# Two-layer mixer and expert network on one core: three weight matrices of the second expert loaded into slots beside the ring, and gate biases summed in the out stage

## What is computed

```
cond = silu(c)
for layer in range(2):
    mod = cond @ ada_w[layer] + ada_b[layer]
    sh_m, sc_m, gt_m, sh_f, sc_f, gt_f = split(mod, 6)
    h = modulate(rms_norm(x, norm_mix[layer]), sh_m, sc_m)
    x = x + gt_m * mixer(h)            # even_mixer, then gla_mixer
    h = modulate(rms_norm(x, norm_ffn[layer]), sh_f, sc_f)
    x = x + gt_f * hier_moe(h)         # top-1 group of 4, top-2 experts in it
# one expert:
hid = silu(h @ w1[e]) * (h @ w3[e]);  y = hid @ w2[e]
```

## Time and profile before

| | |
|---|---|
| median of 3 runs | 2037.02 us (2034.14 to 2037.91) |
| profiled execution, its own time | 2039.77 us |
| its span, first to last instruction | 2037.9 us |
| TensorE busy | 1689.9 us (83%) |
| VectorE, ScalarE busy | 607.2 us (30%), 362.7 us (18%) |
| moved by the DMA engines | 582.33 MB, mean 286 GB/s |
| mean granted TensorE clock | 0.917 of 2.4 GHz |

### The profile page before, as it was taken

How to read it: one execution, slowest core, us unless ns; L and a number is a source line. 1 busy time by engine, 2 the same in 40 slices (tenths; PEclk the granted TensorE clock), 3 DMA queues, 4 the chain that set the end, 5 groups by cost and what they waited for, 6 DMA issues and landing times.

```text
span 2037.9 us, 26620 instructions
## 1 busy us (share of the span) xinstructions
PE 1689.9 (83%) x11304; PEld 1049.5 (51%) x11304; DVE 607.2 (30%) x1546; ACT 362.7 (18%) x817; POOL 74.1 (4%) x80
## 2 busy tenths in 40 slices
PE   6997879877676776999986866786789999899988
PEld 4756754433333333755543533353368884558753
DVE  2657643211111111671321111111142051411192
ACT  1013113100000001222320100000021132311271
POOL 0000100000000001000000000000100000000000
PEclk8997898988888888998898988898899999999999
DMA  9995206999999999764499999999994433046100
GB/s 354 377 295 207 83 2 248 403 428 429 427 429 428 429 428 415 266 238 154 176 417 422 426 429 428 426 427 427 427 337 150 143 139 145 1 149 227 61 1 31
DMA packets 142767, 582.33 MB, mean 286 GB/s; under 512 B 30941, under 2 KB 42333, under 8 KB 117985
## 3 DMA queue, kind: packets, MB, share of 16 engines
q1 hardware_dynamic: 113504, 558.49, 68.0%
q10 hardware_dynamic: 24000, 10.32, 2.0%
q0 software_dynamic: 5184, 12.43, 1.8%
HBM read 571.41 MB, written 13.11 MB: 287 GB/s over the span
## 4 chain that ended last, share of the span: by engine, by line
PE 48%; DMA 38%; DVE 7%; issue 2%; ACT 2%; PEldq 1%; PEld 1%; DVEq 0%; SPq 0%; ACTq 0%
DMA ring<-in_exp_w_dram 35%; PE bank L725 14%; PE bank L714 6%; PE bank L856 6%; PE bank L2100 4%; PE bank L2461 3%; PE bank L2159 2%; PE bank L2451 2%; DMA ring<-in_hawk_w_mem_kv_dram 1%; DMA ring<-in_ada_w_dram 1%; PEldq L167 1%; PE bank L1968 1%; PE bank L2106 1%; DVE pair_probs L3237 1%; DVE pair_probs L3222 1%
## 5 line engine op out<-in xcount | busy, mean ns | idle before, releaser
L2100 PE MATMUL bank<-ring,hidden_room 128*32 128x512 f32 x2048 | 294.1, 698 | 186.6 <-DMA ring<-in_exp_w_dram 184.7
L725 PE MATMUL bank<-hT,ring 128*128 128x256 f32 x1344 | 292.5, 380 | 2.8 <-DVEq L167 1.4
L725 PEld LDWEIGHTS bank<-hT,ring 128*128 128x128 f32 x1344 | 255.5, 190 | 38.7 <-issue 4.0
L2100 PEld LDWEIGHTS bank<-ring,hidden_room 128*32 128x32 f32 x2048 | 64.2, 120 | 341.4 <-DMA ring<-in_exp_w_dram 187.7
L2358 DVE COPY hidden_room<-bank 128x512 f32<-128x512 f32 x64 | 44.3, 692 | 540.2 <-PE bank L2100 540.2
L2159 PE MATMUL bank<-ring,hidden_room 128*32 128x256 f32 x2048 | 159.8, 465 | 52.6 <-DMA ring<-in_exp_w_dram 38.7
L2106 PEld LDWEIGHTS bank<-kc,hidden_room 128*128 128x128 f32 x1024 | 132.9, 203 | 70.6 <-issue 63.1
L2106 PE MATMUL bank<-kc,hidden_room 128*128 128x32 f32 x1024 | 140.3, 282 | 3.0 <-DVE hidden_room L2358 1.6
L2159 PEld LDWEIGHTS bank<-ring,hidden_room 128*32 128x32 f32 x2048 | 74.3, 128 | 105.7 <-issue 59.9
L2265 ACT COPY hidden_room<-bank 128x512 f32<-128x512 f32 x64 | 37.5, 586 | 486.6 <-PE bank L2100 486.6
L714 PE MATMUL bank<-ring,hT 128*128 128x512 f32 (+2 forms) x288 | 116.0, 564 | 0.0
(11 more groups left out here) (589 smaller groups left out, 1838.9 us busy)
## 6 DMA issues: line engine op xcount, KB each, us to landing
ring<-in_exp_w_dram SPq DMA_DIRECT2D x192, 2048.0 KB, 26.6
ring<-in_ada_w_dram SPq DMA_DIRECT2D x24, 2048.0 KB, 14.2
ring<-in_hawk_w_in_dram SPq DMA_DIRECT2D x15, 2048.0 KB, 9.0
ring<-in_even_w_in_dram SPq DMA_DIRECT2D x7, 2048.0 KB, 19.0
ring<-in_gla_w_in_dram SPq DMA_DIRECT2D x6, 2048.0 KB, 20.2
ring<-in_nsa_w_in_dram SPq DMA_DIRECT2D x5, 2048.0 KB, 7.8
ring<-in_even_w_out_dram SPq DMA_DIRECT2D x2, 2048.0 KB, 8.1
expert_out<-kc POOLq DMA_DIRECT2D x8, 512.0 KB, 9.2
```

What stands on the lines that cost most here:

```text
L725: last = nc.tensor.matmul(pair[m // 2][0:rows, (m % 2) * T:(m % 2 + 1) * T], w[:, k, m * P:m * P + rows], src[:, k, :], start=(k == 0), st ...
L2100: last = nc.tensor.matmul(dst[quarters[k % NQ], :], own[:, q, k % 2, k // 2, :], w[:, k, :], start=(k < NQ), stop=(k >= KD - NQ))
```

## The change

1. Parts 4 and 5 of layer 0's expert list (w3 and w2 of expert 1) and part 5 of layer 1's (w2 of expert 1) are taken out of `chunks`. They are loaded by SP in the out stage, after the ring's loads of that stage, into `taken` (part 4) and into a new tile `spare_slot` (part 5). `weights` and `weights_in` take them from there.
2. The gate bias moves from `sum_gate` into `condition_products`: one more 512-column product into the first 32 rows.
3. The first two gate halves are summed and copied ahead of the ranking in place of the first.
4. `mem` becomes a part of `hidden_room`, which is made earlier; the scaled memory has one tile, so the second memory is scaled when the first one has been used.
5. Fillers: four more in the head behind the third condition product; two in place of three ahead of the first expert; four more in the last expert ahead of the wait for its w2.
6. In the branch not taken the first pair is written out.

```diff
+        spare_parts = ((4, 5), (5,))
...
-                chunks.append((KD, FE, [(None, None, A["exp_w1"][layer, e].rearrange("(p k) n -> p (k n)", p=P))]))
-                chunks.append((KD, FE, [(None, None, A["exp_w3"][layer, e].rearrange("(p k) n -> p (k n)", p=P))]))
-                chunks.append((FT, D, [(None, None, A["exp_w2"][layer, e].rearrange("(p k) n -> p (k n)", p=P))]))
+                for part in range(3):
+                    if 3 * e + part not in spare_parts[layer]:
+                        nk, width, src = expert_part(layer, e, part)
+                        chunks.append((nk, width, [(None, None, src)]))
...
-        def condition_products(c, dst, cond):
+        def condition_products(c, dst, cond, bias=None):
             for k in range(KD):
                 g = k % 4
+                if k == 4 and bias is not None:
+                    nc.tensor.matmul(dst[0:32, :], ident[:, 0:32], bias, start=False, stop=False)
...
-                            if j < 2:
+                            if j < 3:
                                 keep_warm(bank[0], 4)
...
+                spare_loads = after.get("spare_loads", ())
+                before = met.n
...
                         fill_ring(sp, c0 + n + more - 1)
+                        if spare_loads:
+                            sp.wait_ge(met.sem, before)
+                        for (to, of), landing in zip(spare_loads, spare_in):
+                            sp.dma_start(to, of).then_inc(landing.up(16), 16)
...
-                            condition_products(c0 + n + j, bank[part_banks[j]], cond).then_inc(chunk_used.up(), 1)
+                            pe.wait_ge(bias_in.sem, bias_in.n)
+                            condition_products(c0 + n + j, bank[part_banks[j]], cond, after["gates"][j]).then_inc(chunk_used.up(), 1)
...
-                    copy_gate(0)
+                    for j in range(2):
+                        copy_gate(j)
...
-                    for j in range(1, len(gate_halves)):
+                    for j in range(2, len(gate_halves)):
                         copy_gate(j)
...
-                        pe.wait_ge(bias_in.sem, bias_in.n)
-                        dst = bank[part_banks[j]][:, :]
-                        nc.tensor.matmul(dst, pick.to_broadcast([P, P]), parts[:, j, :], start=True, stop=False)
-                        nc.tensor.matmul(dst, ident, gate_halves[j], start=False, stop=True).then_inc(picked.up(), 1)
-
-                    sum_gate(0)
+                        nc.tensor.matmul(bank[part_banks[j]][:, :], pick.to_broadcast([P, P]), parts[:, j, :],
+                                         start=True, stop=True).then_inc(picked.up(), 1)
+
+                    for j in range(2):
+                        sum_gate(j)
...
-                    for j in range(1, len(gate_halves)):
+                    for j in range(2, len(gate_halves)):
                         sum_gate(j)
...
+                    n = 3 * e + part
+                    return c0 + n - sum(m < n for m in spare_parts[layer]) + sum(e >= 2 * pair for pair in bounds)
...
+                    if n in spare_parts[layer]:
+                        landing = spare_in[spare_parts[layer].index(n)]
+                        pe.wait_ge(landing.sem, landing.n)
+                        return
...
                     nc.scalar.copy(memory_kT[name].rearrange("p m t -> p (m t)"), key_bank[:, :]).then_inc(memory_kept.sem, 1)
+                    if n + 1 < len(bounds):
+                        scale_memory(act, after_pair[bounds[n + 1]])
...
+                                    if closing and q == 1:
+                                        keep_warm(bank[3], 4)
                                     weights_in(pe, pair, i, q, 2)
...
-                            keep_warm(bank[2], 3)
+                            keep_warm(bank[2], 2)
...
-                            for name in after_pair.values():
-                                scale_memory(act, name)
+                            if after_pair:
+                                scale_memory(act, after_pair[bounds[0]])
...
-                mem = sb(st, "mem", [P, TT, D]) if layer else None
...
+                room = sb(st, "hidden_room", [P, 3072])
+                mem = room[:, 1024:3072].rearrange("p (t d) -> p t d", t=TT) if layer else None
+                spare = [sb(st, "spare_slot", [P, SLOT])[:, :]]
+                if not layer:
+                    spare.insert(0, taken[:, :, :, :].rearrange("p t n d -> p (t n d)"))
+                spare_loads = [(to, expert_part(layer, n // 3, n % 3)[2]) for to, n in zip(spare, spare_parts[layer])]
```

More of the change, by code:

```diff
@@ L267, in program, with expert_part @@
         memory_at = ({}, {4: "hawk", 11: "nsa"})
+        spare_parts = ((4, 5), (5,))
+        def expert_part(layer, e, part):
+            nk, width = ((KD, FE), (KD, FE), (FT, D))[part]
+            return nk, width, A[("exp_w1", "exp_w3", "exp_w2")[part]][layer, e].rearrange("(p k) n -> p (k n)", p=P)
         def experts(layer):
@@ L408, in program @@
         consts_in, tables_in = signal("consts_in"), signal("tables_in")
+        spare_in = [signal(f"spare{n}_landed") for n in range(2)]
         gates = [memory_kv, sb(st_first, "gates1", [P, 2, D])]
@@ L1834, in _, with experts_stage @@
                     nc.vector.memset(best[:, 0, 0, 0:1], 0.0).then_inc(gate_free.up(), 1)
-        def experts_stage(layer, gates, xn, gain, shift, parts, gate_halves, taken, mem, final_row, final_row_in, next_gain, next_shift):
+        def experts_stage(layer, gates, xn, gain, shift, parts, gate_halves, taken, mem, room, spare, final_row, final_row_in, next_gain, next_shift):
             c0 = first[f"experts{layer}"]
@@ L1938, in weights @@
                 def weights(pair, q):
-                    return [slot(chunk_of(2 * pair + q, part)) for part in range(3)]
-                def weights_in(pe, pair, i, q, part):
+                    found = []
+                    for part in range(3):
+                        n = 3 * (2 * pair + q) + part
+                        if n in spare_parts[layer]:
+                            nk = expert_part(layer, n // 3, part)[0]
+                            found.append(spare[spare_parts[layer].index(n)].rearrange("p (k n) -> p k n", k=nk))
+                        else:
+                            found.append(slot(chunk_of(n // 3, part)))
+                    return found
+                def weights_in(pe, pair, i, q, part):
+                    n = 3 * (2 * pair + q) + part
+                    if n in spare_parts[layer]:
+                        landing = spare_in[spare_parts[layer].index(n)]
+                        pe.wait_ge(landing.sem, landing.n)
+                        return
                     c = chunk_of(2 * pair + q, part)
@@ L1949, in experts_stage @@
                         signalled, n = frees_from[part]
-                        freed[chunk_of(e, part)] = (signalled.sem, n(e))
+                        if 3 * e + part not in spare_parts[layer]:
+                            freed[chunk_of(e, part)] = (signalled.sem, n(e))
                 used0 = chunk_used.n
@@ L3395, in program @@
                 xn = sb(st, "xn_kept", [P, TT, D])
+                room = sb(st, "hidden_room", [P, 3072])
[4 more added lines that the diff above has]
+                spare_loads = [(to, expert_part(layer, n // 3, n % 3)[2]) for to, n in zip(spare, spare_parts[layer])]
                 final_row, final_row_in = parts[:, 2:4, :].rearrange("p a n -> p (a n)"), signal("gain_row_in")
                 out_stage(first[("even_out", "gla_out")[layer]], [(0, KD)], hT, gates[layer][:, 0, :],
-                          {"gain": mod[layer][:, 2, :], "shift": mod[layer][:, 3, :], "dst": hT, "xn": xn, "gates": gate_halves, "mem": mem, "junk": taken})
+                          {"gain": mod[layer][:, 2, :], "shift": mod[layer][:, 3, :], "dst": hT, "xn": xn, "gates": gate_halves, "mem": mem, "junk": taken, "spare_loads": spare_loads})
                 next_gain, next_shift = (col("hawk_norm_2"), None) if layer else (mod[1][:, 0, :], mod[1][:, 1, :])
-                experts_stage(layer, gates[layer], xn, mod[layer][:, 2, :], mod[layer][:, 3, :], parts, gate_halves, taken, mem, final_row, final_row_in,
+                experts_stage(layer, gates[layer], xn, mod[layer][:, 2, :], mod[layer][:, 3, :], parts, gate_halves, taken, mem, room, spare, final_row, final_row_in,
                               next_gain, next_shift)
```

11 lines of the change are left out of this document (5 added, 6 removed).

## The result

Six runs of the changed kernel have a median of 2027.16 us (2024.85 to 2029.22), six of the kernel before beside them 2034.32 (2031.64 to 2037.91): ratio 0.995, interval [0.9936, 0.9964]. By the ratio the change makes the kernel some 10 us faster (7 to 13); the two medians lie 7.2 us apart. The forecast was 22 us and 2015.0 us, with a range up to 2025; 2027.2 lies 2 us above it. The profiled execution of after took 2028.43 us (span 2026.6, granted clock 0.922).

What follows compares the result with a forecast made beforehand. Load stream bounds both expert stages: when it starts and its chunks of 4.90 us. −9.8 − 4.9 − 0.2 + 0.8 − 3.3 − 4.6 = −22.0 us, from a median of 2037.0 to 2015.0 us; range 2009.5 to 2025.

Steps and rivals of the forecast that it cites:

- the loads: Expert stages: extra loads fill holes in the stream, two chunks fewer in layer 0 (−9.8 us), one in layer 1 (−4.9).
- rival C: Expert stages: extra loads miss the hole or the ring runs dry; up to 14.7 us lost, 2029.7 us; chance 0.09.
- rival D: Load stream itself becomes slower, 8.8 us per per cent; at 3% 2041.3 us; chance 0.03.
- The 358 GB/s: The skill's bound for HBM loads: 5.9 us a chunk, sum 2.9 us larger; the forecast used the measured rate instead.
- Closing, −4.6: End of each expert stage: four fillers ahead of the last matrix's landing speed its products, −2.3 us per layer.
- Head, −3.3: Head: four more fillers keep the clock up, so projections start earlier; −3.3 us, bounds 0 and −3.45.
- Busy 1.7 us longer, the engine … should hold the level of 2.4 GHz: 1.6 + 2.4: Head: full clock saves 1.6 us on the fourth condition product, 2.4 on the 32 narrow products; 4.0 before the cut.
- rival A: Head and closings: fillers do not lift the clock; gain falls by 3.3 + 4.6 to 14.1, 2022.9 us; chance 0.26.
- half of it to win: Head: the 32 narrow products took 4.82 us, of which full clock would save half, 2.4 us.
- Starts of the expert stages, −0.2 and +0.8: Moved gate biases, fewer summing products and one filler less shift the experts' start: layer 0 −0.2 us, layer 1 +0.8.
- Rival B: Out stages: added bias products start the experts late, +3 to +5 us, about 2019 us; chance 0.10.
- The unrolled pair in the untaken branch … 0: Branch not taken behind the experts' code: writing out its first pair was put at 0 us.

Runs made afterwards that it cites:

- experiment 1: The changed kernel run again, no edit: 2028.51 us, 0.9944 of the kernel before.
- experiment 4: The changed kernel without its three extra loads, all parts through the ring again: 2042.55 us, 1.0014 of the kernel before.
- experiment 9: The changed kernel plus eight never-run filler matmuls in layer 0's branch not taken, run a second time: 2019.08 us, 0.9907 of the kernel before.
- experiment 11: The changed kernel without its three extra loads, plus eight never-run fillers in layer 0's branch not taken: 2033.29 us, 0.9983 of the kernel before.
- experiment 10: The three loads alone: head and closing fillers and bias products as before the change, sixteen never-run fillers as padding: 2021.93 us, 0.9916 of the kernel before.
- The kernel before with padding: The kernel before plus only 170 never-run filler matmuls in layer 0's branch not taken: 2046.21 us, 1.0045 of the kernel before.
- experiment 8: The padded kernel with gate biases and order of the gate sums as before the change: 0.9903 of the kernel before.
- experiment 2: The changed kernel plus eight never-run filler matmuls in layer 0's branch not taken, first run: 2022.44 us, 0.9915 of the kernel before.
- experiment 6: The padded kernel without the four closing fillers of each layer, as many matmuls put into branches not taken: 0.9935 of the kernel before.
- The padded kernel: The changed kernel plus eight never-run filler matmuls in layer 0's branch not taken, run twice: 0.9915 and 0.9907 of the kernel before.

## Why the prediction failed by half

**What bounded the kernel, and the loads: right.** −14.7 us was forecast; experiments 1 and 4 give 14.3, experiments 9 and 11 15.5, experiment 10 alone 17.1 (14 to 20). By the profiles, first expert product to the last matrix's products went from 458.14 to 448.64 us in layer 0, −9.5 for two chunks of 4.90, and in layer 1 from 469.37 to 463.65, −5.7 for one. The ring did not run dry (rival C), and the rate stayed: 431 GB/s at 500 us (rival D). The 358 GB/s that the prediction took from the Trainium skill (DMA: Bandwidth & Descriptors, Where 436 GB/s comes from) does not agree with this trace either.

**Closing, −4.6: the mechanism right, the worth too high.** 3.64 became 1.93 us in both layers, and last products to final sum 7.40 to 5.07 and, in layer 1, 7.60 to 5.51: −2.3 and −2.1 in the profile. In the four profiles without fillers the same products take anything from 1.93 to 3.64 us, so 2.3 is the most that a layer gives, not what every execution gives.

**Head, −3.3: wrong.** The step "Busy 1.7 us longer, the engine … should hold the level of 2.4 GHz: 1.6 + 2.4" held in its first half alone. The timeline of after, against the earlier trace rows:

```profile
30.78 1.92 PE L444 MATMUL bank<-ring,cond 128*32 128x512 f32 x16 [0.67 <-DMA ring<-in_ada_w_dram]
33.41 5.66 PE L451 MATMUL bank<-kc,mod_parts 128*128 128x1 f32 x32 [0.70 <-ACT mod_parts L500]
...
42.22 4.15 PE L735 MATMUL bank<-hT,ring 128*128 128x256 f32 x18 [0.38 <-PEq L167]
```

The condition product fell to 1.92 us as forecast, but the 32 one-column products behind it took 5.66 us, more than the 4.82 of before. Two stretches with TensorE busy throughout say why, the granted clock being the last figure but two:

```profile
34.00:36.00 2.00, 2.00 (x16) 2.00 (x15) 0.00 (x0) 0.00 (x0) 0.00 (x0) 0.73 1.06 389
36.00:38.00 2.00, 2.00 (x11) 2.00 (x10) 0.00 (x0) 0.00 (x0) 0.00 (x0) 0.50 1.05 386
```

The clock fell to the 1.2 GHz level while the engine was busy with them. That is what rival A named; it was right for this half of the head and wrong for the condition product and the closings. The price was wrong as well. Where the clock held, as in experiment 1's profile, the narrow products took 3.73 us (their row of the timeline, and the first of the two stretches):

```profile
33.49 3.73 PE L451 MATMUL bank<-kc,mod_parts 128*128 128x1 f32 x32 [0.70 <-ACT mod_parts L500]
34.00:36.00 2.00, 2.00 (x20) 2.00 (x20) 0.00 (x0) 0.00 (x0) 0.00 (x0) 1.00 1.05 388
```

So "half of it to win" was 1.1 us of the 4.82 and not 2.4. Over all profiles the narrow products take 3.73 to 5.79 us with the head's filler (three of ten under 3.8) and 3.73 to 4.89 without, and the projections start at 39.95 to 43.27 us with it (mean 41.7 of ten) and at 40.17 to 42.95 without (mean 42.0 of four). One profile's 42.85 was taken for a fixed cost; the start varies by 3 us with either code. The kernel before with padding, which has no filler there, started 2.7 us earlier than before all the same, by the clock alone: 1.92 us for the condition product after 2.05 us of idling, 3.73 us, start at 40.17. Head, closings and starts together were −7.3; experiment 11 has −3.5 (0.8 to 6.1).

**Starts of the expert stages, −0.2 and +0.8: too small to tell in the time.** Layer 0's turned even mixer (first copy of the turned tile) to first expert product went from 65.72 to 64.34 us, but the same code gives 62.65 to 65.44 in other profiles, and experiment 8, with the biases as before, 62.67. In layer 1 the sign was wrong: from the first condition product of the out stage to the first expert product it took 28.04 us before and 26.73 after, 1.3 us less where 0.8 more was forecast. The four profiles with the biases as before have 27.77 to 28.04, eight of the ten with the change 26.73 to 26.75 (28.26 and 28.32 in experiments 2 and 6). Rival B is not seen; its price of 3 to 5 us is hardly larger than layer 0's scatter of 2.8.

**"The unrolled pair in the untaken branch … 0": the step that failed most.** It was priced by the work that it runs, none, where its size moves all later code of TensorE. It cost 5.9 us by experiments 1 and 2, where the forecast had 0. The sum with the measured terms is −15.5 (loads) − 3.5 (small parts) + 5.9 (pause) = −13.1 us; the ratios of the changed kernel say 10.2 and 11.4, with about 3 us of uncertainty each. No rival had this mechanism; the list had only costs of work that is run.

The padded kernel, at 0.9915 and 0.9907, beats both kernels, for eight fillers that are never run. It is made for this very length of code: any later edit of TensorE's program ahead of the turn moves the place again. Undoing the peel gives as much (0.9917) but would need the branch to read the spare slots in its loop.

## What to carry to other kernels

Code that is never run isn't free where it moves code that is: count an edit's instructions too, and when a stage between two unchanged landmarks has become some microseconds longer, with an engine idle on "issue" in the middle of a run of equal instructions, look at the instruction packets of the DMA view around it. A cheap test is a handful of instructions in a branch not taken; a guard, not tried here, would be a place for the jump where the engine waits for another one anyway. And a stretch whose length hangs on the granted clock is priced from several executions, not from the one that was profiled.

## What was not expected of the hardware

Two fetched blocks of code came some 6 us apart in all fourteen profiles while the load stream ran (393 and 422 GB/s in the two half microseconds shown), the first engine work behind the jump came 2.55 us or more after the first block's packet started, and 170 matmuls that are never executed made a kernel of 2036 us slower by 9 us. The granted clock was 0.73 and then 0.50 in two stretches of after in which TensorE was 2.00 of 2.00 us busy with one-column products, and 1.00 in the first of them in experiment 1's profile of the same code.
